# Modulation chunks of a recurrent decoder step, moved from the mixers' inverse steps to their late steps

## The reference, cut to what matters

```
mods = (jax.nn.silu(c) @ ada_w + ada_b).reshape(B, 3, 3, 1, D_MODEL)      # ada_w: 1024 x 9216 in each layer
modulate(t, i) = t * (1.0 + mods[:, i, 1]) + mods[:, i, 0]
x = residual(x, 0, _swiglu(modulate(x, 0), ...), 0.5)
proj = modulate(x, 1) @ w_in
o_rw, o_gla, o_ml = rwkv7(proj), gated linear attention(proj), mLSTM(proj)
x = residual(x, 1, concatenate([o_rw, o_gla, o_ml]) @ w_out, 1.0)
x = residual(x, 2, _swiglu(modulate(x, 2), ...), 0.5)
```

## Time and profile before

| | |
|---|---|
| time, median of 3 runs | 1710.79 us (1704.85 to 1715.14) |
| the profiled execution's own time | 1713.31 us |
| its span | 1711.5 us |
| TensorE busy | 1634.3 us, 95% |
| VectorE, ScalarE, GpSimd busy | 55%, 39%, 11% |
| TensorE's mean granted clock | 0.953 |

### The profile page before, as it was taken

One profiled execution on the slowest core, in us unless ns is written; L12 is line 12 of the kernel. 1 busy time (PEld: TensorE's weight loads), 2 busy tenths in 40 slices (PEclk: granted clock), 3 DMA queues, 4 the chain that ended last, 5 costly groups with the idle time before them and its releaser, 6 DMA issues.

```text
span 1711.5 us, 32995 instructions
## 1 busy us (share of the span) xinstructions
PE 1634.3 (95%) x14132; PEld 1502.8 (88%) x14132; DVE 945.5 (55%) x1607; ACT 663.8 (39%) x959; POOL 180.9 (11%) x251
## 2 busy tenths in 40 slices
PE   5999999999999999999999999999899989999997
PEld 2999998988777779999989999989878767899996
DVE  1544545585653676555465445466846457755544
ACT  2233334463323345433354333355542233643333
POOL 1000011100202131000120000110020223100011
PEclk9999999999986799999999999999998769999999
DMA  8766465433442164444655544654311215544441
GB/s 313 267 225 211 156 227 190 157 111 111 132 137 88 63 233 148 154 150 148 246 197 209 187 153 153 244 169 148 111 63 54 82 38 172 201 152 148 148 149 67
DMA packets 92513, 270.23 MB, mean 158 GB/s; under 512 B 27184, under 2 KB 29648, under 8 KB 92112
## 3 DMA queue, kind: packets, MB, share of 16 engines
q1 hardware_dynamic: 87952, 265.50, 45.4%
q10 hardware_dynamic: 4416, 2.62, 0.6%
HBM read 261.83 MB, written 6.26 MB: 157 GB/s over the span
## 4 chain that ended last, share of the span: by engine, by line
PE 82%; DVE 10%; DMA 4%; ACT 2%; issue 1%; SPq 0%; POOL 0%; DVEq 0%; ACTq 0%; POOLq 0%
PE psV L2039 12%; PE psV L2040 12%; PE psV L2041 12%; PE psA L2039 9%; PE psA L2041 9%; PE psA L2040 9%; DMA raw<-weights_dram 4%; PE psV L800 3%; DVE wlo L2357 2%; PE psC L2054 2%; PE psY L2054 1%; DVE PJ L1517 1%; PE psV L2064 1%; ACT whi L2215 1%; PE psV L1621 1%
## 5 line engine op out<-in xcount | busy, mean ns | idle before, releaser
L2357 DVE TENSOR_TENSOR wlo<-raw,whi 128x1024 fp32r<-128x1024 f32 x334 | 412.7, 1239 | 400.6 <-ACT whi L2215 398.0
L2215 ACT ACTIVATE whi<-raw 128x1024 fp32r<-128x1024 f32 x334 | 352.3, 1056 | 327.0 <-PE psV L2041 302.1
L2039 PE MATMUL psA<-XH,whi 128*128 128x320 f32 x1120 | 350.8, 313 | 11.9 <-DVE wlo L2357 10.3
L2041 PE MATMUL psA<-XH,wlo 128*128 128x320 f32 x1120 | 347.9, 311 | 0.0
L2040 PE MATMUL psA<-XL,whi 128*128 128x320 f32 x1120 | 347.9, 311 | 0.0
L2039 PE MATMUL psV<-XH,whi 128*128 128x320 f32 x848 | 267.1, 315 | 0.2
L2040 PE MATMUL psV<-XL,whi 128*128 128x320 f32 x848 | 263.8, 311 | 0.0
L2041 PE MATMUL psV<-XH,wlo 128*128 128x320 f32 x848 | 263.7, 311 | 0.0
L2039 PEld LDWEIGHTS psA<-XH,whi 128*128 128x128 f32 x1120 | 212.3, 190 | 16.0 <-issue 13.1
L2039 PE MATMUL psV<-HH,whi 128*128 128x320 f32 x704 | 217.5, 309 | 0.0
L2041 PE MATMUL psV<-HH,wlo 128*128 128x320 f32 x704 | 217.5, 309 | 0.0
(11 more groups left out here) (404 smaller groups left out, 1903.0 us busy)
## 6 DMA issues: line engine op xcount, KB each, us to landing
raw<-weights_dram SPq DMA_DIRECT2D x408, 512.0 KB, 3.3
own<-weights_dram SPq DMA_DIRECT2D x56, 512.0 KB, 6.0
in_xh<-weights_dram SPq DMA_DIRECT2D x6, 512.0 KB, 4.8
in_xl<-weights_dram SPq DMA_DIRECT2D x6, 512.0 KB, 4.6
raw<-weights_dram SPq DMA_DIRECT2D x8, 256.0 KB, 3.8
in_hl<-weights_dram SPq DMA_DIRECT2D x4, 512.0 KB, 5.6
ZS<-st_rw_dram SPq DMA_DIRECT2D x2, 768.0 KB, 4.6
S<-st_gla_dram ACTq DMA_DIRECT2D x2, 768.0 KB, 4.8
```

Source lines behind the costliest of these rows:

```text
L2039: mm(out, split_hi(n)[:, k], hi[:, kt], start=first, stop=False)
L2041: return mm(out, split_lo(n)[:, k], hi[:, kt], start=False, stop=last)
L2215: activation(split_hi(n), buffer(DENSE[n]), ACT.Copy).then_inc(hi_done, 1)
L2357: tt(split_lo(n), buffer(DENSE[n]), split_hi(n).bitcast(F32), ALU.subtract).then_inc(lo_done, 1)
```

## The change

Layer 0 has five of its seven groups in the late steps instead of three, layer 1 all three instead of two. `LATE` has 20 places instead of 12, of which eight are named `ada_` (four before), and these are left out in a layer with fewer than four late groups instead of fewer than three.

```
-LATE = ("rw ml ada gl rw ml ada gl ml ada_ rw gl ml ada rw gl ml ada ada_ gl ada rw ml ada_ gl ada rw ml ada gl ada_ ml ada rw fold "
-        "gl rw ml su mix rs rw rs su hi.0 rs lo.0 rw hi.1 rw hi.2 lo.1 early.0 rw lo.2 early.1 rw").split()
-IN_LATE = (3, 2)
+LATE = ("rw ml ada ada_ gl rw ml ada_ ada gl ml ada ada_ rw gl ml ada rw gl ml ada ada_ gl ada_ ada rw ml ada ada_ gl ada rw ml "
+        "ada gl ada ada_ ml ada ada_ rw ada fold gl rw ml su mix rs rw rs su hi.0 rs lo.0 rw hi.1 rw hi.2 lo.1 early.0 rw lo.2 early.1 rw").split()
+IN_LATE = (5, 3)
...
-    out += spread([(step, 1) for step in together], ada_groups(in_tail[:-IN_LATE[L]]))
+    out += spread([(step, 1) for step in together], ada_groups(in_tail[:-IN_LATE[L]]) if in_tail[IN_LATE[L]:] else [])
...
-        if name == "fold" or name == "ada_" and IN_LATE[L] < 3:
+        if name == "fold" or name == "ada_" and IN_LATE[L] < 4:
```

## The result

After takes 1727.47 us (median of 7 runs, 1719.74 to 1729.89), before 1710.79 (7 runs, 1702.29 to 1715.14) beside it. The ratio is 1.0096, with a 95% interval of 1.0062 to 1.0130: slower by 0.96%, some 16.5 us, where 9.1 were forecast.

What follows compares the result with a forecast made beforehand. TensorE, busy for 95% of the span, was taken to bound the kernel. Layer 0 late +14.2, inverse -5.9, layer 1 late +2.8, inverse -2.0 gave +9.1 us: from the median 1710.79 to 1720 us, 0.53% slower, range 1707 to 1730.

Steps and rivals of the forecast that it cites:

- the inverse of layer 0: Layer 0's inverse steps: 7 chunks and 2 folds fewer, plus one fold behind line 847, give back 5.9 us (4.2 to 8).
- The three waits: Layer 0's late steps: TensorE waits about 5 us behind line 1591, 0.5 behind line 1621, 1.5 behind line 1350.
- 14.2 - 0.6: Layer 0's late steps: terms sum to 14.2 us longer; a fold going from behind line 847 gives 0.6 back.
- The fold behind line 847: Layer 0: one more fold goes from behind line 847, giving back 0.6 us within the 5.9.
- A quarter off 5.9: Lower bound of layer 0's gain: TensorE waits for VectorE where fewer chunks remain, so a quarter may be lost, leaving 4.2.
- the first itself: Behind line 1591: next group's first chunk waits for ScalarE's copy, starting 5.57 us after the previous chunk; 4.6 us net.
- 1.2 for lines 1331 to 1342 at the lower clock: Layer 0, behind the idle TensorE: these lines may run at the lower clock, 0 to 2.3 us more; half taken.
- Layer 1: Inverse steps give back 2.0 us (1.0 to 3.3); late steps, with four chunks and one fold more, take 2.8.
- Rival 1: Late steps: added chunks bring the clock back up; all 59 us lifted would give 22 us, 1698. Chance 0.10.
- Rival 2: Late steps: added chunks mostly fill gaps, leaving 2.7 us, 1713.5, no difference that can be told. Chance 0.35.
- Rival 3: Late steps: second chunks of pairs wait for their weights; half of eight pairs, 6 us more, 1726. Chance 0.05.

Runs made afterwards that it cites:

- e3: After with three layer-0 chunks moved one place, so no group's last chunk stands right ahead of the next group's first; 1707.99 us, ratio 0.9995 to before.
- e8: After with one layer-0 chunk, group B's last, moved one place earlier, ahead of line 884; 1709.85 us, ratio 1.0030 to before.
- e12: After with one layer-0 chunk, group C's first, moved one place later, behind line 1342; 1714.70 us, ratio 1.0055 to before.
- e11: Before with one layer-0 chunk moved from behind line 1591 to behind line 1342; 1717.33 us, ratio 1.0045 to before.
- e9: Before with one layer-0 chunk moved one place later, to stand with another ahead of line 884; 1705.88 us, ratio 0.9991 to before.
- e7: Layer 0 as in e3, layer 1 as in before; 1708.41 us, ratio 1.0013 to before.
- e5: Before with two layer-0 chunks one place later, and 56 unread small products filling the resulting wait behind line 1591; outputs wrong; 1717.08 us, ratio 1.0064.

## Why the forecast came out as it did

**Right.** Up to line 829 the inverse of layer 0 gave back 6.7 us for 5.3 of the forecast's 5.9 (the other 0.6 was a fold behind line 847), within its bounds, at a clock of 1.00 where before had 0.94. The three waits are where and as long as the forecast put them: C0 5.56 us behind B3 (forecast 5.57), 0.50 behind line 1621 (0.5), 1.61 behind line 1350 (about 1.5). From line 829 to line 899 layer 0 takes 12.7 us more in the profile (forecast 14.2 - 0.6 = 13.6). The direction hung on the places where two groups meet, and e3, which has none of them, shows it: without them there is no loss.

**Small errors of the sum.** The fold behind line 847 doesn't go; after has it ahead of that line, at 483.38 us. What goes uncounted is a chunk that before has behind line 839 at 490.88 us, at the lower clock. The two leave 0.4 us. A quarter off 5.9 is 4.4, not 4.2.

**Luck in the range.** 1727.5 lies inside 1707 to 1730 only because the upper end holds 6 us for pairs that wait for their weights, of which layer 0's late steps show none. Without them the bounds of the terms end at +12.9, and the change cost 16.5.

**Mis-sized: what the clock takes where the groups meet.** The terms that hang on the waits were 4.9 for the first itself (in the sum as 4.6, with the work around it), 1.2 for lines 1331 to 1342 at the lower clock, 0.5 and 1.6: 8.2 of the 9.1 us. e3, which has none of the three, lies 17 us below after. The place that failed is "Behind an idle TensorE the clock may already be down: 0 to 2.3, I take half". In the profile of after it was the upper bound, 2.36 us. I priced only the three lines behind the wait, and held all further lines for unchanged since they ran at 0.50 before as well. The table has the rest: between after and e3 the span at full clock differs by 1.5 us, and what the clock took by 16.7. Not all of that is shown to follow from the waits. e3 also has a second chunk ahead of line 884, and e8 and e12, which take the first wait away with two chunks and with one there, give back 11 and 7 us. That the mere place of a chunk moves the clock (e11, 0.45%) stood in the sum at nothing. Where in an execution the loss falls no profile here shows: those of before and after have mean granted clocks of 0.953 and 0.954.

**Mis-sized: the ground it stood on.** The profiled execution of before was taken as 2.5 us over the median, and the sum of one execution as the difference of the medians. Between the two profiles the difference is 6.4 us, near the sum of 9.1; over all runs it is 16.5. An execution's clock moves its time by more than any term of the sum.

**Layer 1.** Up to line 829 it gave back nothing (-1.0 forecast, +0.7 measured, at 0.94 instead of 1.00), and the rest cost nothing (forecast +2.8, less 1.0 for the fold at 1315.64 us; measured -0.1): two misses that cancel.

**Rival 1** (the added chunks lift the clock) did not come true for the change, but its ground is sounder than its chance of 0.10. One chunk moved out of the stretch ahead of line 1331 costs 0.45% (e11), all of it clock by the table. The chance was set by single chunks that did not lift a clock already down; that chunks might keep it from falling was not weighed. More of them, though, bought nothing (e9).

The Trainium skill (TensorE: Matmul & The Clock Gate, section What's actually happening) says that the slow clock is the default, that activity releases it, and that the same kernel may run more or fewer products at the slow clock from run to run. The traces agree in part: the clock is down behind the idle 4.92 us of after, and the 87 runs of before range from 0.941 to 0.963, but it is also down from 523 to 546 us of before, where TensorE is busy for 22.71 of 23.00 us. By the rule for an idle engine the forecast should have taken the upper bound behind the wait, 2.3 us, and not half of it.

**Rival 2** (the chunks fill gaps, 1713.5) has the time of e3 and e7, not of the change: once the groups don't meet, 20 chunks in the late steps take no more time than 12 that can be told. That they fill gaps isn't shown, since e3's span at full clock is 6 us over before's. **Rival 3**: the waits of TensorE in after show no chunk that waits for its weights in layer 0's late steps; the only waits for a chunk are the three for MR.

**Still open.** How the loss divides between the waits and the places of the chunks; why e3's span at full clock is 6 us over before's while its clock gives 8 back; whether a filled wait keeps the clock (e5); and why e12, with a clock like before's, isn't faster. No kernel here beats before by more than can be measured.

## What to carry to other kernels

When a list is filled up with pieces from elsewhere, look at what two pieces that now stand side by side share: two groups through one PSUM bank put a copy on another engine between them, and behind which instructions that copy stands decides how long the wait is. Price a wait on the engine that bounds the kernel at its length at least, and look at what its clock does behind it. Test it by moving one piece by one place, and run a control that moves a piece and keeps the waits as they are: here such a move alone cost 0.45%. Before a difference of 1% is explained from two profiles, see how far two executions of one kernel lie apart.

## What was not expected of the hardware

- One chunk of 0.64 us, moved behind lines 1331 to 1342 with no work or wait added, made the kernel slower by 0.45% (0.21 to 0.69); the span at full clock stayed at 1628.0 us, and what the clock took rose from 78.4 to 84.7.
- A wait of 4.7 to 4.8 us put into before, by moving two or three chunks, cost 0.81 and 0.85%, some 14 us; the nearest kernels without the wait cost 0.45% (e11) and 0.61% (e6).
- Runs of one kernel differ by 24 us of 1708, and the time follows the mean granted clock (correlation -0.82 over 87 runs of before).
